# Moving the weight tiles and the moving tiles of a two-layer kernel by 64 bytes each in SBUF

## The reference, cut to what matters

```python
h = h + mixer(rms_norm(h)) ;  h = h + ffn(rms_norm(h))     # twice, with different mixers
q, k, v, f_logit = split(h @ w_in)                         # 2048 x 6160
up = h @ w_up ;  ... ;  (silu(gate) * val) @ w_down        # 2048 x 11264, 5632 x 2048
```

## The kernel before, in words

| tiles | start modulo 256 before | after |
|---|---|---|
| raw | 128 | 128 |
| whi, wlo | 128 | 192 |
| xres | 128 | 192 |
| xs, mix, hid2 | 192 | 128 |
| folded_t, qk, qk_n, v_t, v_tok, probs, sq_hi, sq_all, head_o | 192 | 128 |
| ident, mean_d, mean_hr, tap_g, tap_v, silu_g, hid | 128 | 64 |
| sq_sum, rstd, sq_x | 64 | 0 |
| g_q, g_k, g_vtok, g_attn, g_qs, g_state | 224 | 160 |
| narrow_sb | 32 | 224 |

## Time and profile before

### The profile page before, as it was taken

The page is one execution under the profiler, slowest core; times in us unless marked ns, Lnnn a source line. Parts: engine busy times, 40 slices in busy tenths (PEclk is TensorE's granted clock), DMA queues, the critical chain, the costliest instruction groups (busy, mean ns, idle before and its releaser), DMA issues.

```text
span 2255.5 us, 38934 instructions
## 1 busy us (share of the span) xinstructions
PE 2239.5 (99%) x13138; PEld 1966.5 (87%) x13138; DVE 1617.6 (72%) x2394; ACT 1225.7 (54%) x1614; POOL 54.5 (2%) x78
## 2 busy tenths in 40 slices
PE   7999999999999999999999999999999999999999
PEld 6888888888888888888888888888888888888888
DVE  7877777888888888555567687777666666764554
ACT  6777765655555555444465577655444444443333
POOL 1111100000000000000000000000000000000000
PEclk9999999999999999999999999999999999999999
DMA  6655555565555555655555554555555555556664
GB/s 206 194 176 182 182 175 186 188 196 188 193 195 192 189 187 187 204 194 188 195 164 184 169 177 166 166 194 193 190 192 189 192 195 191 191 192 200 204 198 138
DMA packets 118602, 421.99 MB, mean 187 GB/s; under 512 B 13773, under 2 KB 15973, under 8 KB 118544
## 3 DMA queue, kind: packets, MB, share of 16 engines
q1 hardware_dynamic: 113760, 413.19, 55.2%
q0 software_dynamic: 2048, 5.42, 0.9%
q10 hardware_dynamic: 2736, 2.58, 0.4%
HBM read 419.01 MB, written 3.70 MB: 187 GB/s over the span
## 4 chain that ended last, share of the span: by engine, by line
PE 98%; ACT 1%; DVE 1%; DMA 1%; issue 0%; SPq 0%; DVEq 0%
PE acc L392 63%; PE acc L397 31%; PE b_score L445 0%; PE b_turn L450 0%; DMA xres<-xt 0%; PE b_mean L456 0%; PE b_mean L435 0%; PE b_mean L436 0%; PE b_val L442 0%; PE b_mean L457 0%; PE b_score L444 0%; PE b_mean L458 0%; DMA raw<-wstream 0%; ACT xs L844 0%; ACT whi L716 0%
## 5 line engine op out<-in xcount | busy, mean ns | idle before, releaser
L716 ACT ACTIVATE whi<-raw 128x1024 fp32r<-128x1024 f32 x783 | 825.4, 1058 | 820.9 <-PE acc L397 815.1
L1040 DVE TENSOR_TENSOR wlo<-raw,whi 128x1024 fp32r<-128x1024 f32 x783 | 958.3, 1227 | 386.5 <-ACT whi L716 383.5
L392 PE MATMUL acc<-xs,whi 128*128 128x512 f32 x4344 | 1129.7, 394 | 2.2 <-DVE wlo L1040 1.8
L392 PEld LDWEIGHTS acc<-xs,whi 128*128 128x128 f32 x4344 | 764.1, 188 | 124.8 <-DVE wlo L1040 3.5
L397 PEld LDWEIGHTS acc<-xs,wlo 128*128 128x128 f32 x4344 | 607.2, 188 | 64.7
L397 PE MATMUL acc<-xs,wlo 128*128 128x256 f32 x4344 | 619.2, 277 | 0.0
L392 PE MATMUL acc<-hid,whi 128*128 128x512 f32 x1408 | 359.9, 391 | 0.0
L1046 DVE TENSOR_REDUCE folded_t<-acc 128x256 f32<-128x512 f32 x336 | 231.1, 688 | 124.2 <-PE acc L397 112.8
L392 PEld LDWEIGHTS acc<-hid,whi 128*128 128x128 f32 x1408 | 247.2, 188 | 37.9
L397 PEld LDWEIGHTS acc<-hid,wlo 128*128 128x128 f32 x1408 | 194.2, 188 | 19.9
L397 PE MATMUL acc<-hid,wlo 128*128 128x256 f32 x1408 | 197.5, 276 | 0.0
(11 more groups left out here) (195 smaller groups left out, 1000.4 us busy)
## 6 DMA issues: line engine op xcount, KB each, us to landing
raw<-wstream SPq DMA_DIRECT2D x783, 512.0 KB, 3.3
decay_row<-decay_scratch POOLq DMA_DIRECT2D x16, 128.0 KB, 3.7
out<-xres ACTq DMA_DIRECT2D x16, 128.0 KB, 3.0
xres<-xt SPq DMA_DIRECT2D x3, 512.0 KB, 8.4
dist_scratch<-bias_scratch POOLq DMA_DIRECT2D x8, 192.0 KB, 4.7
toeplitz<-dist_scratch POOLq DMA_DIRECT2D x8, 128.0 KB, 3.9
xres<-xt SPq DMA_DIRECT2D x2, 256.0 KB, 4.5
raw<-wstream SPq DMA_DIRECT2D x2, 256.0 KB, 5.8
```

The costliest lines, as they stand in the source:

```text
L392: pe.matmul(acc[bank_no][:, :], w_hi, x[:, kc, :, :].rearrange("p a s -> p (a s)"), start=opens, stop=False)
L716: act.activation(whi[slot][:, :], raw[slot][:, :], ACT.Copy).then_inc(hi_ready, 1)
L1040: dve.tensor_tensor(wlo[slot][:, :], raw[slot][:, :], whi[slot][:, :], ALU.subtract).then_inc(lo_ready, 1)
```

## The change

```diff
@@ -41,7 +41,8 @@
 BLOCKS = 8
 PHASE = 256
-X_AT = 192
+X_AT = 128
+W_AT = 192
 UW = BLOCKS * P
@@ -107,6 +108,7 @@
         raw = [sb(f"raw{i}", [P, UW]) for i in range(RING)]
+        sb("skipped_w", [P, (W_AT - nc.sbuf_base) % PHASE // 4])
         whi = [sb(f"whi{i}", [P, UW], F32R) for i in range(RING)]
         wlo = [sb(f"wlo{i}", [P, UW], F32R) for i in range(RING)]
```

## The result

The changed kernel takes 2281.79 us (median of four runs, 2281.45 to 2282.12) against 2256.87 us: a ratio of 1.0111, 95% interval 1.0099 to 1.0123. It is 1.1% slower, 24.9 us. The forecast was no change. The time lies in the wide range given, and next to rival A's half price (2282 us).

What follows compares the result with a forecast made beforehand. TensorE's own pace was taken to bound the kernel, as it hardly ever waits. Five terms of 0 gave a profiled 2257.3 us, or 2257.0 us as median, no change (0.40); the range was 2225 to 2308 us.

Steps and rivals of the forecast that it cites:

- rival A: Moving stream meets the next weights' load in L392 and L397: up to 8.3 ns a pair, 2307 us, half 2282; chance 0.29.
- Steps (a) to (c): Unused tiles, the splits' weight tiles moved to 192 modulo 256, and xres moved to 192 for its transfers: each cost 0.
- Step (d): Small matmuls, whose tiles keep their mutual distances but change absolute phase: about 350 passes, 1 us either way, taken as 0.
- Step (e): Moving tiles against weights in 6264 pairs, 64 bytes above to 64 below: bounded by -108 and +50 us, taken as 0.
- CATCH-UP: Experiments' theory that the moving stream catches the next weights' load: about 2270 us at distance 128, 2257 or less at 32.
- Rival B: Moving tiles starting at a multiple of 128 save L392's odd 2.1 ns a pair: 13 us, 2244 us; chance 0.23.
- Rival C: The pairs' whole surplus over their columns hangs on the moving tile's start: 108 us faster, 2149 us; chance 0.08.

Runs made afterwards that it cites:

- m3: TensorE alone, no full kernel: bfloat16 and plain float32 matmuls at eight distances of moving tile from weights; 215.8 to 215.9 ns for 512 bfloat16 columns or a 256-column float32 pass.
- e3: Kernel before with moving tiles at 64 and weights still at 128 modulo 256, the changed kernel's distance of 192; 2281.6 us, ratio 1.0109.
- e4: Weights at 192 as in the changed kernel, moving tiles at 0 modulo 256, keeping the distance of 64 of the kernel before; 2256.6 us, ratio 0.9999.
- e9: Kernel before with the unequal lead-in groups of long stretches made plain sixes; ten runs: one 2256.9 us, four 2270.2 to 2272.4, five 2285.0 to 2286.6.
- m1: TensorE alone, no full kernel: fp32r matmuls of 512 and 256 columns at 16 distances, without lead-in groups; 344.4 to 353.3 ns a pair, 348.9 at distance 64.
- m2: TensorE alone again, fp32r rounds with and without lead-in groups; at distance 64 342.2 ns a pair behind them and 346.7 without, at 192 346.7 and 350.0.
- e10: Changed kernel with the unequal lead-in groups of long stretches made plain sixes; 2281.76 us, ratio 1.0115.
- e6: Kernel before with the low weights alone moved to distance 192 by 128 unused bytes, high weights left at 64; 2291.0 us, ratio 1.0155.

## Why the prediction was wrong

- **What bounds the kernel** was right: only TensorE's pace could move the end, and the time moved by that pace alone. Steps (a) to (c) held: L718 at 1058 ns, L1042 at 1228, the idle in front of L394 at 2.2 us.
- **Step (d)** held: the plain float32 passes of 256 columns take 215.8 ns at any distance tried (m3), and the small matmuls' shares of the chain are as before. (Counted by groups there are 392 such passes and not 350, 1.2 us at 3 ns each, which changes nothing.)
- **Step (e) failed.** It had the right relation (distance modulo 256 from 64 to 192, everything else unchanged, shown by e3 and e4) and the right bounds (-108 to +50 us), and then took 0 because the fast stretch of the earlier trace rows was the nearest row: "a distance that is the same modulo 128". Nothing in the trace said that 128 is the period. e3 and e4 show that it is 256 or more: 64 and 192 have the same residue modulo 128 and differ by 4.4 ns a pair. I should have taken the nearest row only for a distance that the trace shows.
- **Rival A** had the right side: 4.4 ns a pair of the 8.3 that it allowed. That the time meets its half price, 2282 us, is luck. That price was for half of the matmuls caught and the rest at the old pace, but in the changed kernel all steady rounds have the new one. The 8.3 itself was read from chain pieces rounded to 0.01 us; the slow rhythm at the old addresses is 348.9 against 342.2 ns, 6.7 a pair (e9). Its mechanism, a moving stream that runs into the load, is not shown as it was put. CATCH-UP, its exact form, failed at 32 and 128. What is shown is that no engine but TensorE is needed (m1), that the distance decides which steady rhythms turn up (342.2 at best for 64, 346.7 for 192, 350.0 for 0), and that at 64 the groups ahead can decide which of them is run (m2, e9). The pace that the heads show in the earlier trace rows was the clue: same addresses, two paces. I used it as a bound and didn't ask what else than the address sets the pace. For the long stretches at distance 64 the code had one answer, the lead-in groups; in the heads, which have none, the stream goes back to 1.37 and 0.68 us without them.
- **Rival B** fails: with the moving tiles at 0 modulo 256 and the distance kept at 64 (e4), a start at a multiple of 128 gives no gain. **Rival C** fails too: no distance of sixteen, behind or without the lead-in, is below 342.2 ns a pair, nor do ten pairs of split ones.
- **The Trainium skill**, "TensorE: Matmul & The Clock Gate", section "Back-to-back issue gap", has a formula for the isolated gap of a warm matmul, from which 215.8 and 109.2 ns follow for 512 and 256 columns. m3's streams agree to 0.1 ns for bfloat16. For fp32r no run came near. The sentence of the Trainium skill on separate read ports (same page, "Step-by-step: what each phase is for") is in keeping with m3 for bfloat16; for fp32r the measured paces at different distances speak against leaning on it.

What stays open is the inner cause: why distance 64 has a rhythm of 342.2 and no other distance tried, and whether the pattern repeats after 256 bytes or after more. Also open are why the changed kernel reaches 346.7 ns without the groups (e10) where TensorE alone needs them, and why e6 changes its rhythm from stretch to stretch behind the same groups. The lead-in's effect was measured, not explained.

## What to carry to other kernels

For a stream like this one, fp32r with a new block of weights for each matmul and 512 and 256 columns in groups of six, start from the moving tile 64 bytes above the weight tiles modulo 256 and all weight tiles at one residue, and don't reason modulo 128. For another pattern measure it anew: matmuls of a single kind ran best at other distances. For bfloat16 and float32 placement made no difference, in matmuls of a single kind; mixed ones weren't tried. An fp32r stream can settle in a slow rhythm with the same instructions, so compare stretches of one length in the chain of waits, and where the pace differs look at how the stretch is entered. A placement is only measured together with its lead-in, and one run of it may not show all of its rhythms.

## What the runs showed of the hardware that I had not expected

- TensorE alone, with all else idle, runs the same six-and-six pattern at 342.2 to 353.3 ns a pair, depending on the distance in steps of 16 bytes and, at distances 64 and 192, on the groups ahead of it.
- A rhythm lasts: 24 rounds of twelve matmuls at 346.7 ns at distance 64 without a change, while 342.2 was open to it.
- The best distance of each kind is not that of the mix: 512-column matmuls alone run best at distances 0 and 240 (226.7 ns) and 256-column ones at 16, 112 and 192 (113.3 ns), but pairs at 240 take 348.9 to 351.1 ns.
- One full kernel can change rhythm within an execution: e6 between 344.5, 349 and 352 ns a pair, e9 between 342.2, 348.9 and 346.7.
- Without the lead-in groups one program had three times, 2257, 2271 and 2286 us, at a granted clock of 1.00.
